# Bidirectional SSD scan on one core: PSUM banks split four and four, state decays given to Pool, row loads, turned-x copies and row scaling moved

## The chip, the cores and the metric

The kernel runs on one core of a Trainium2 chip. The metric is the device time of one execution in microseconds, the median of the runs. PE is TensorE, ACT is ScalarE, DVE is VectorE, Pool is GpSimd, and SP issues the loads of the weights.

## The reference

A first block of a transformer (AdaLN modulation, neighbourhood attention beside a bidirectional state-space scan "SSD", then a mixture of 16 experts), then two plain layers with attention and an MLP. All is fp32, 512 tokens of width 1024, and 256 tokens of context. The change lies in the SSD part, whose core is this:

```python
def _ssd_scan(xs, dt, A, Bm, Cm, h0, return_y):       # 4 groups of 8 heads, head size 64, state 128, chunks of 128
    ...
    states = jnp.einsum('bclgn,bcgrl,bclgrp->bcgrpn', Bc, decay_to_end, x)
    chunk_decay = jnp.exp(a_cs[..., -1]).astype(xs.dtype)
    def step(h, inp):
        dec, st = inp
        return dec[..., None, None] * h + st, h
    ...
    y_diag = jnp.einsum('bcgls,bcgrls,bcsgrp->bclgrp', cb, Lm, x)
    y_off = jnp.einsum('bclgn,bcgrpn,bcgrl->bclgrp', Cc, jnp.moveaxis(h_prev, 0, 1), jnp.exp(a_cs).astype(xs.dtype))
```

Before the scan, the projections of x, B and C pass a convolution over 5 tokens and a SiLU; after it, y is multiplied by SiLU(z) and normalised by root mean square within its group.

## The kernel before

Each engine has a program of its own, and semaphores join them: `up(sem, key)` counts up and names the event, `wait_ge(*at(key))` waits for it. Each engine runs its instructions in the order of its program. The programs are Python generators. `weave(main, filler, per)` mixes two of them at a fixed rate; `pace(main, filler, plan)` mixes them by a list, entry k being how many steps of the filler go ahead of step k of main. All engines use the same mix, so a step of PE has its counterpart on ACT, DVE and Pool.

The 8 banks of PSUM are handed out in turn within a list: `open_bank(pe, key, pool)` takes the bank of that list that was taken longest ago and makes PE wait until its earlier contents are read (the key `free`). Main work takes from `PA = [3, 4, 5, 6, 7]`, filler work from `PG = [0, 1, 2]`.

The SSD runs over groups g = 0 to 3. Main for group g is `*_chunks(g)`, 15 steps:

- Steps 1 to 5 (n = 0 to 4) are the sweep over states. A step has two states, one of each direction; the ten are m = 0 to 9 and are called st0 to st9 here, each one matmul of 128x512 (line 1039). Its right side `xd` is x times a weight (`weigh`, line 1028): even m on DVE, odd m on Pool. DVE then forms the new state as the earlier one times a decay (line 1212) plus the bank (line 1215).
- Steps 6 to 15 (n = 0 to 9) are the output. `act_exponents(n)` makes decay exponents for half a chunk, 8 activations (line 1124) on rows that the ACT queue has loaded from DRAM (`load_rows`, line 1104); `act_decays(n)` takes their exponential (line 1133), after the exponents of n+1; `pool_first` multiplies by C·B (line 1306), which gives M(n); PE's `pe_second(n)` (line 1072) needs M(n). For odd n it also makes the two state terms `yo` (line 1079). `dve_second`, `pool_second` (lines 1316 to 1320) and `dve_join` (line 1277) put y together; the join frees the bank of y.

The filler for group g+1 is `*_proj(g+1)`, 8 steps F1 to F8. F1 to F4 are the convolutions of x, i = 0 to 3. In each, PE projects (line 720, two banks), ACT copies both banks to a padded row (lines 730 and 733), DVE does one product and four multiply-adds (lines 754 and 758), ACT takes SiLU (lines 739 and 742), and PE turns tile i-1 (line 307, two banks), of which DVE copies one part (line 965) and ACT the other (`act_turn_x`, line 935). F5 to F8 make z (line 295, copied with SiLU at line 956). By the rate 0.56 they fall so: steps 1, 2, F1, 3, 4, F2, 5, 6, F3, 7, 8, F4, 9, F5, 10, 11, F6, 12, 13, F7, 14, 15, F8. For group 3 the filler is the q and k projections of two groups of heads (lines 1531 and 1724, copied by ACT at lines 1538 and 1773), and main does its first three steps without filler.

The norm of the group before is finished inside the sweep. `dve_scale_z` and `pool_scale_z` (line 1192) scale its rows by `rstd`, which ACT helps to make (`act_rstd`, lines 327 and 329); PE turns them (`pe_finish`, part 0 and 1), ACT copies the turned tiles (`act_finish`, line 1176) and sends them to DRAM (line 1178, key `yD`). Group 3's own finish comes after its last step and two empty steps. The next stage begins with `PHASE_C`, a wait on all engines but PE for that finish, its last `yD` among the keys; then ACT and DVE copy the tokens into another order (`act_by_blocks`, line 1731, and `dve_by_blocks`, line 1736), on which PE's v projection waits.

Of the kernel before, what the change touches and what calls it, by code (L numbers as in the profile page):

```python
# [178 lines left out]
def build(nc, A, out):  # L179
    ctx = ExitStack()  # L180
    with ctx:
# [66 lines left out]
        PALL, PA, PG = list(range(8)), [3, 4, 5, 6, 7], [0, 1, 2]  # L248
        rings = [PS]
# [476 lines left out]
        def act_conv(act, nm, i, ti, dx, dc, before):  # L726
# [7 lines left out]
                *up(S("act_pad"), ("free", (nm, i, 2)), ("pad", (nm, i))))  # L734
            act.wait_ge(*at("acc", (nm, i)))
# [196 lines left out]
        def act_turn_x(act, g, i):  # L932
            key = ("tx", g, i, 4)
            act.wait_ge(*at("full", key))
            act.activation(xs2[g % 2][:, 4:6, i * 128:(i + 1) * 128], r3(PS.of(key)[:, 0:256], 128), ACT.Copy, bias=0.0, scale=1.0).then_inc(  # L935
                *up(S("act_xs"), ("free", key), ("xs", g, i, 4)))

        def act_proj(act, g):
            for i in range(4):
                prev = ("tx", g, i - 2, 4) if i > 1 else ("tx", g - 1, i + 2, 4)  # L940
                before = [("full", prev)] if g or i > 1 else []
                if g == 0 and i == 1:
                    before = [("full", ("BF", 3, 2))]
                act_conv(act, ("x", g), i, 4 * g + i, xsF[i % 2][:, 0:512], xsF[i % 2][:, 512:768], before)
                if g > 1 and i == 1:
                    act.wait_ge(*at("gone", g - 2, "pool"))
                    act.wait_ge(*at("gone", g - 2, "pe"))
                if i:
                    act_turn_x(act, g, i - 1)
                yield  # L950
# [80 lines left out]
        def pe_chunks(pe, g, pool):  # L1031
            xsT, BT = xs2[g % 2], BT2[g % 2]
            for m, (d, n, c) in enumerate(SWEEP):
# [6 lines left out]
                if d:  # L1040
                    if n in (2, 3) and g:
                        pe_finish(pe, g - 1, n - 2, pool)
                    yield
# [66 lines left out]
        def act_exponents(act, g, n):  # L1110
# [7 lines left out]
            for d in range(2):  # L1118
# [7 lines left out]
                if d == 0:  # L1126
                    for e in range(2):
                        load_rows(act, g, n + 1, e)
# [6 lines left out]
        def act_chunks(act, g):  # L1135
            for d in range(2):
                load_rows(act, g, 0, d)
            for n in range(5):
                if n == 0 and g:
                    act_rstd(act, ("ssd", g - 1), ssy, 4)  # L1140
                if n in (2, 3) and g:
                    act_finish(act, g - 1, n - 2)
                if n == 4:
                    act_exponents(act, g, 0)
                yield
# [48 lines left out]
        def dve_chunks(dve, g):  # L1194
            for m in range(3):
                weigh(dve, 0, g, m)
            for m, (d, n, c) in enumerate(SWEEP):
# [9 lines left out]
                else:  # L1207
                    cd = bc(r3(cdec, 64)[:, c, 32 * d + 8 * g:32 * d + 8 * g + 8], 64)
                    dve.wait_ge(*at("h", g, d, n - 1))
                    if g == 0 and n == 1 and d == 0:  # L1210
                        dve.wait_ge(*at("cd"))
                    dve.tensor_tensor(r3(dst, 64), r3(H_[:, SLOT[d][n - 1], :], 64), cd, ALU.mult).then_inc(*up(S("dve_state")))
                    dve.wait_ge(*at("full", key))
                    dve.wait_ge(*now(S("dve_state")))
                    dve.tensor_tensor(dst, dst, b, ALU.add).then_inc(*up(S("dve_state"), ("free", key), ("h", g, d, n), *keys))
                if d:
                    if n == 0 and g:
# [64 lines left out]
        def pool_chunks(pool, g):  # L1282
            for m in range(3):
                weigh(pool, 1, g, m)
            for m, (d, n, c) in enumerate(SWEEP):
                weigh(pool, 1, g, m + 3)
                if d:
                    if n == 0 and g:
# [1646 lines left out]

        def sp_program(sp):
# [25 lines left out]
        def pe_program(pe):  # L2962
# [31 lines left out]
        def act_program(act):  # L2994
# [9 lines left out]
            weave(main, chain(act_na_qk(act, 0), act_na_qk(act, 1)), 0.57)  # L3004
# [27 lines left out]
        def dve_program(dve):  # L3032
# [10 lines left out]
            weave(main, chain(dve_na_qk(dve, 0), dve_na_qk(dve, 1, 0)), 0.57)  # L3043
# [22 lines left out]
        def pool_program(pool):  # L3066
# [7 lines left out]
            weave(main, chain(pool_na_qk(pool, 0), pool_na_qk(pool, 1)), 0.57)  # L3074
# [58 lines left out]
```

## Time and profile before

| | us |
|---|---|
| median of 3 runs | 4042.74 (4036.76 to 4048.11) |
| the profiled execution | 4034.85 |
| its span, first to last instruction | 4032.9 |
| PE busy | 3663.4 (91%) |
| DVE, ACT, POOL busy | 1137.1, 782.8, 450.8 |
| stretch of the change, first st0 of group 0 to the v projection | 303.9 to 801.2 |

Times in the trace are microseconds from the first instruction. Engine busy times overlap, so they don't add up to the span. The chain that ended last is PE for 53% of the span and DMA for 18%. A row of the timeline gives the start, the length of the run of like instructions, the instruction and its count, and in brackets the idle time ahead of it with what ended it. An fp32 matmul shows as two instructions.

### The profile page before, as it was taken

How to read it: one execution, taken by the hardware profiler on the slowest of the kernel's cores; microseconds unless marked ns; L12 is line 12 of the kernel's file. 1: busy time of each engine (PE TensorE's matmuls, PEld its weight loads, DVE VectorE, ACT ScalarE, POOL GpSimd, SP SyncE). 2: the span in 40 equal slices, each digit the busy share in tenths (PEclk: the TensorE clock that was granted, in tenths of full speed). 3: DMA queues.
4: the chain of work that ended last, by engine and by line, in shares of the span. 5: the costliest groups of instructions: out<-in, count | busy, mean ns of one | idle time of the engine just before them, and what ended most of it. 6: DMA issues, size and time to landing. Idle time of an engine off the chain costs nothing.

```text
span 4032.9 us, 32976 instructions
## 1 busy us (share of the span) xinstructions
PE 3663.4 (91%) x12600; PEld 1762.2 (44%) x12600; DVE 1137.1 (28%) x2594; ACT 782.8 (19%) x1786; POOL 450.8 (11%) x405
## 2 busy tenths in 40 slices
PE   6898888899999888888888888899999999999999
PEld 3354444444444443333233334555444445554444
DVE  2335444434310220311101114443221134432211
ACT  2024344322310210000000003332110123221100
POOL 1001223412100000000000002100221011012210
PEclk8899898999999989999999998999999999999999
DMA  7322223211212569999999992102222120022220
GB/s 253 125 75 75 79 63 94 87 37 50 79 63 88 189 250 409 409 409 409 409 409 409 409 398 73 37 27 84 83 72 80 51 90 32 28 97 69 84 71 34
DMA packets 302153, 634.08 MB, mean 157 GB/s; under 512 B 32499, under 2 KB 145763, under 8 KB 301743
## 3 DMA queue, kind: packets, MB, share of 16 engines
q1 hardware_dynamic: 240480, 591.96, 39.1%
q10 hardware_dynamic: 61519, 40.02, 3.5%
q8 instruction: 102, 1.67, 0.2%
q14 instruction: 52, 0.43, 0.0%
HBM read 625.50 MB, written 10.24 MB: 158 GB/s over the span
## 4 chain that ended last, share of the span: by engine, by line
PE 53%; DMA 18%; DVE 3%; SPq 1%; ACT 1%; issue 1%; POOL 0%; DVEq 0%; ACTq 0%
PE psum L295 26%; DMA arena<-in_w_exp_up_dram 7%; DMA arena<-in_w_exp_gate_dram 7%; PE psum L1531 6%; DMA arena<-in_w_exp_down_dram 4%; PE psum L2799 4%; PE psum L2763 4%; PE psum L2304 4%; PE psum L1359 2%; PE psum L1387 1%; PE psum L2784 1%; PE psum L2253 1%; PE psum L1368 1%; SPq L264 1%; PE psum L2694 1%
## 5 line engine op out<-in xcount | busy, mean ns | idle before, releaser
L295 PE MATMUL psum<-arena 128*128 128x512 f32 (+1 forms) x3200 | 1309.8, 568 | 17.1 <-ACT arena L935 11.9
L295 PEld LDWEIGHTS psum<-arena 128*128 128x128 f32 x3200 | 612.4, 193 | 699.2 <-issue 660.3
L2304 PE MATMUL psum<-arena 128*64 128x512 f32 x3072 | 696.5, 598 | 148.8 <-DMA arena<-in_w_exp_up_dram 76.2
L2304 PEld LDWEIGHTS psum<-arena 128*64 128x64 f32 x3072 | 234.4, 137 | 592.1 <-issue 571.6
L1531 PE MATMUL psum<-arena 128*128 128x512 f32 x768 | 352.8, 614 | 0.0
L720 PE MATMUL psum<-arena 128*128 128x512 f32 (+1 forms) x768 | 274.5, 517 | 1.3 <-ACT arena L538 1.3
L1531 PEld LDWEIGHTS psum<-arena 128*128 128x128 f32 x768 | 147.5, 196 | 193.2 <-issue 192.4
L1465 DVE CUSTOM_DVE_ANT_0 arena<-psum,arena 128x512 f32<-128x512 f32 (+3 forms) x224 | 114.0, 546 | 384.5 <-PE psum L1359 376.3
L2842 POOL TENSOR_SCALAR arena<-arena 128x512 f32<-128x512 f32 x88 | 138.6, 1576 | 696.2 <-ACT arena L2821 696.2
L720 PEld LDWEIGHTS psum<-arena 128*128 128x128 f32 x768 | 152.5, 201 | 125.4 <-issue 114.7
L2848 DVE SCALAR_TENSOR_TENSOR arena<-arena 128x512 f32<-128x512 f32 x88 | 66.2, 752 | 426.6 <-POOL arena L2842 426.6
L1407 ACT ACTIVATE arena<-arena 128x512 f32<-128x512 f32 (+3 forms) x224 | 134.3, 601 | 134.3 <-DVE arena L1465 133.7
L2369 DVE TENSOR_TENSOR arena<-arena,psum 128x512 f32<-128x512 f32 x32 | 22.0, 689 | 462.0 <-PE psum L2304 462.0
L2799 PE MATMUL psum<-arena 128*128 128x512 f32 x352 | 152.0, 592 | 0.0
L2763 PE MATMUL psum<-arena 128*128 128x512 f32 x352 | 151.7, 592 | 0.0
L2821 ACT ACTIVATE arena<-psum 128x512 f32<-128x512 f32 x88 | 52.5, 597 | 509.7 <-PE psum L295 478.2
L1368 PE MATMUL psum<-arena 128*128 128x128 f32 x576 | 85.7, 277 | 55.9 <-DVE arena L1472 30.7
L1542 POOL TENSOR_TENSOR arena<-arena 128x512 f32<-128x512 f32 x48 | 61.3, 1277 | 608.3 <-ACT arena L1538 595.2
L307 PE MATMUL psum<-arena 128*128 128x128 f32 (+3 forms) x442 | 67.6, 300 | 53.4 <-ACT arena L730 18.9
L1368 PEld LDWEIGHTS psum<-arena 128*128 128x128 f32 x576 | 68.4, 142 | 107.6 <-DVE arena L1472 38.1
L2763 PEld LDWEIGHTS psum<-arena 128*128 128x128 f32 x352 | 66.6, 189 | 84.7 <-issue 84.7
L2206 POOL TENSOR_TENSOR arena<-arena 128x128 f32<-128x128 f32 x32 | 12.9, 433 | 809.1 <-PE psum L307 593.2
(276 smaller groups left out, 3022.9 us busy)
## 6 DMA issues: line engine op xcount, KB each, us to landing
arena<-in_w_exp_gate_dram SPq DMA_DIRECT2D x128, 1024.0 KB, 18.6
arena<-in_w_exp_up_dram SPq DMA_DIRECT2D x128, 1024.0 KB, 18.6
arena<-in_w_exp_down_dram SPq DMA_DIRECT2D x128, 1024.0 KB, 18.8
arena<-in_w_in_dram SPq DMA_DIRECT2D x64, 1024.0 KB, 5.3
arena<-in_w_up_dram SPq DMA_DIRECT2D x88, 512.0 KB, 4.8
arena<-in_w_ada_dram SPq DMA_DIRECT2D x24, 1024.0 KB, 7.9
arena<-in_w_down_dram SPq DMA_DIRECT2D x20, 1024.0 KB, 4.9
arena<-acs_scratch ACTq DMA_DIRECT2D x64, 256.0 KB, 4.5
```

The source lines that it names most:

```text
L295: mm = pe.matmul(shaped(b, l, r), l, r, start=kt == 0, stop=kt == nkt - 1)
L307: t = pe.transpose(b[0:m, c * k:(c + 1) * k], x, ident[0:k, 0:k])
L720: mm = pe.matmul(b[:, 0:z - a], wt(nm, kt, 512)[:, i * 128:(i + 1) * 128], HT[:, kt, a:z], start=kt == 0, stop=kt == 7)
L1359: pe.matmul(b[:, 0:u.nk], J.queries(u, a, z), J.keys(u, a, z), start=True, stop=True).then_inc(*up(S("pe_score"), ("full", ("s2", J.id, i, ...
L1368: t = pe.transpose(b[:, 128 * j:128 * j + 128], J.score(i, c)[:, 128 * j:128 * j + 128], ident)
L1407: act.activation(J.score(i, c), J.score(i, c), ACT.Exp, bias=sv2(i, c)[:, 0:1], scale=-1.0, accum_out=sv2(i, c)[:, 1:2]).then_inc(*up(S("a ...
L1465: dve.tensor_tensor_reduce(out=J.score(i, c), in0=PS.of(("s2", J.id, i, c))[:, 0:u.nk], in1=J.table(u, c), scale=-J.scale(u), scalar=3.0e3 ...
L1531: mm = pe.matmul(b, wt(nm, kt, 256)[:, i * 128:(i + 1) * 128], src[:, kt, 0:512], start=kt == 0, stop=kt == 7)
L2304: mm = pe.matmul(banks[n][64 * j:64 * j + 64, :], lhs[:, kt, 64 * j:64 * j + 64], w, start=kt == 0, stop=kt == 2 * nkb - 1)
L2763: mm = pe.matmul(banks[i], actT[:, kt, i * 128:(i + 1) * 128], wt(nm, kt, 512), start=kt == 0, stop=kt == 21)
L2799: mm = pe.matmul(b, actT[:, kt, i * 128:(i + 1) * 128], wt(nm, kt, 512), start=kt == 0, stop=kt == 21)
L2842: pool.tensor_scalar(accs3[n % 4], pads3[n % 4][:, 0:512], w3(L, 0, ti_of(s, i)), None, ALU.mult).then_inc(*up(S("pool_acc"), ("acc3", L, n)))
```

## The change

1. **Banks.** In the four main stretches of the SSD and their fillers the lists are `PA1 = [4, 5, 6, 7]` and `PG1 = [0, 1, 2, 3]`.
2. **State decays.** The product of the earlier state and the decay, 8 per group, is issued by Pool into the new slot, and DVE only adds the bank.
3. **Turned x.** ACT copies its part of turned tile i-1 between the pad copies and the SiLU of convolution i, no longer after the SiLU.
4. **Row scaling and finish.** `act_rstd`, `dve_scale_z` and `pool_scale_z` move from n = 0 to n = 1; `pe_finish` and `act_finish` from n = 2, 3 to n = 3, 4 (on ACT ahead of the exponents of n = 0).
5. **Row loads.** `act_exponents(n)` issues both row loads for n+1 after its 8 activations, no longer after the first 4.
6. **Group 3.** `pace` with `PLAN0` in place of the rate 0.57. F1 to F5 and F7 stay where they were among the steps; F6 goes ahead of step 14, and F8 ahead of the second empty step, so ahead of group 3's finish and no longer behind it.

```diff
+        PA1, PG1 = [4, 5, 6, 7], [0, 1, 2, 3]
...
             act.activation(pad[:, 518:774], PS.of((nm, i, 2))[:, 0:256], ACT.Copy, bias=0.0, scale=1.0).then_inc(
                 *up(S("act_pad"), ("free", (nm, i, 2)), ("pad", (nm, i))))
+            if between:
+                between()
...
-                act_conv(act, ("x", g), i, 4 * g + i, xsF[i % 2][:, 0:512], xsF[i % 2][:, 512:768], before)
...
-                if i:
-                    act_turn_x(act, g, i - 1)
+                act_conv(act, ("x", g), i, 4 * g + i, xsF[i % 2][:, 0:512], xsF[i % 2][:, 512:768], before,
+                         (lambda: act_turn_x(act, g, i - 1)) if i else None)
...
-                    if n in (2, 3) and g:
-                        pe_finish(pe, g - 1, n - 2, pool)
+                    if n in (3, 4) and g:
+                        pe_finish(pe, g - 1, n - 3, pool)
...
-                if d == 0:
-                    for e in range(2):
-                        load_rows(act, g, n + 1, e)
+            for d in range(2):
+                load_rows(act, g, n + 1, d)
...
-                if n == 0 and g:
+                if n == 1 and g:
                     act_rstd(act, ("ssd", g - 1), ssy, 4)
-                if n in (2, 3) and g:
-                    act_finish(act, g - 1, n - 2)
+                if n in (3, 4) and g:
+                    act_finish(act, g - 1, n - 3)
...
-                    dve.tensor_tensor(r3(dst, 64), r3(H_[:, SLOT[d][n - 1], :], 64), cd, ALU.mult).then_inc(*up(S("dve_state")))
                     dve.wait_ge(*at("full", key))
-                    dve.wait_ge(*now(S("dve_state")))
+                    dve.wait_ge(*at("hc", g, d, n))
                     dve.tensor_tensor(dst, dst, b, ALU.add).then_inc(*up(S("dve_state"), ("free", key), ("h", g, d, n), *keys))
...
                 weigh(pool, 1, g, m + 3)
+                if n:
+                    H_ = (hf, hb)[d]
...
+                    pool.wait_ge(*at("h", g, d, n - 1))
...
+                    pool.tensor_tensor(r3(H_[:, SLOT[d][n], :], 64), r3(H_[:, SLOT[d][n - 1], :], 64), cd, ALU.mult).then_inc(
+                        *up(S("pool_hc"), ("hc", g, d, n)))
                 if d:
-                    if n == 0 and g:
+                    if n == 1 and g:
                         pool_scale_z(pool, g - 1)
...
+        PLAN0 = [0, 0] + [1, 0, 1, 0, 1, 0, 1, 1, 1, 0] + [1, 1]
...
-                weave(pe_chunks(pe, g, PA), pe_proj(pe, g + 1, PG), 0.56)
-            main = pe_chunks(pe, 3, PA)
+                weave(pe_chunks(pe, g, PA1), pe_proj(pe, g + 1, PG1), 0.56)
+            main = pe_chunks(pe, 3, PA1)
...
-            weave(main, chain(pe_na_qk(pe, 0, PG), pe_na_qk(pe, 1, PG)), 0.57)
+            pace(main, chain(pe_na_qk(pe, 0, PG1), pe_na_qk(pe, 1, PG1)), PLAN0)
```

## Rows read from the trace of the kernel before

**Rows 1.** Waits of PE, 303 to 801 us: total us, times, longest.

```profile
PE psum L307 <- ACT arena L730: 18.9, 6, 5.7
PE psum L1072 <- POOL arena L1306: 12.1, 8, 2.8
PE psum L295 <- ACT arena L935: 11.9, 3, 4.0
```

**Rows 2.** Timeline of PE, group 1: start, length, instructions, [idle before, releaser].

```profile
444.19 2.08 PE L1039 MATMUL psum<-arena 128*128 128x512 f32 x2 [3.97 <-DVE arena L1215]
...
477.24 0.69 PE L307 MATMUL psum<-arena 128*128 128x128 f32 x2 [5.66 <-ACT arena L730]
478.26 1.94 PE L1072 MATMUL psum<-arena 128*128 128x64 f32 x8 [0.33 <-POOL arena L1306]
...
501.75 8.84 PE L295 MATMUL psum<-arena 128*128 128x512 f32 x16 [3.97 <-ACT arena L935]
...
521.69 1.00 PE L1072 MATMUL psum<-arena 128*128 128x64 f32 x8
...
537.21 1.97 PE L1072 MATMUL psum<-arena 128*128 128x64 f32 x8 [2.76 <-POOL arena L1306]
```

**Rows 3.** Timeline of ACT and its queue in the same stretch.

```profile
448.55 0.69 ACT L1176 ACTIVATE arena<-psum,arena 128x512 f32<-128x512 f32 x1 [0.46 <-ACT arena L1176]
...
466.87 0.94 ACTq L1104 DMA_DIRECT2D arena<-acs_scratch  x2
...
471.20 1.28 ACT L1124 ACTIVATE arena<-arena 128x128 f32<-128x128 f32 x4 [2.07 <-DMA arena<-acs_scratch]
...
476.07 0.63 ACT L1133 ACTIVATE arena<-arena 128x512 f32<-128x512 f32 x1
```

**Rows 4.** Timeline of DVE in the same stretch.

```profile
437.88 4.86 DVE L758 SCALAR_TENSOR_TENSOR arena<-arena 128x772 f32<-128x772 f32 x4
...
460.05 4.20 DVE L758 SCALAR_TENSOR_TENSOR arena<-arena 128x772 f32<-128x772 f32 x4
...
504.59 0.69 DVE L1277 TENSOR_TENSOR arena<-psum,arena 128x512 f32<-128x512 f32 x1 [2.47 <-POOL arena L1320]
...
522.00 0.69 DVE L1277 TENSOR_TENSOR arena<-psum,arena 128x512 f32<-128x512 f32 x1 [6.20 <-POOL arena L1320]
```

**Rows 5.** Groups of instructions, 303 to 801 us: busy us, mean ns | idle.

```profile
L1028 POOL TENSOR_TENSOR arena<-arena 128x512 f32<-128x512 f32 x18 | 22.3, 1254 | 33.7 <-PE psum L1039 33.7
L1212 DVE TENSOR_TENSOR arena<-arena 128x512 f32<-128x512 f32 x32 | 22.2, 695 | 0.0
...
L1192 POOL TENSOR_SCALAR arena<-arena 128x512 f32<-128x512 f32 x8 | 13.6, 1708 | 27.2 <-DVE arena L322 27.2
```

**Rows 6.** Timeline of PE at the start of group 3.

```profile
689.54 2.05 PE L1039 MATMUL psum<-arena 128*128 128x512 f32 x2 [6.18 <-POOL arena L1028]
...
697.46 7.03 PE L1531 MATMUL psum<-arena 128*128 128x512 f32 x16
...
715.77 1.10 PE L1072 MATMUL psum<-arena 128*128 128x64 f32 x8 [2.59 <-POOL arena L1306]
```

**Rows 7.** Timeline of POOL at the start of group 3.

```profile
684.65 3.39 POOL L1192 TENSOR_SCALAR arena<-arena 128x512 f32<-128x512 f32 x2 [7.25 <-DVE arena L322]
```

**Rows 8.** Timeline of PE at the end of group 3.

```profile
784.00 3.65 PE L307 MATMUL psum<-arena 128*128 128x128 f32 x16 [8.00 <-POOL arena L1192]
...
801.23 14.00 PE L295 MATMUL psum<-arena 128*128 128x512 f32 x32 [1.58 <-issue]
```

**Rows 9.** Timeline of ACT and its queue at the end of group 3.

```profile
776.03 0.39 ACT L1773 ACTIVATE arena<-psum 128x256 f32<-128x256 f32 x1 [2.85 <-PE psum L1724]
...
789.82 0.33 ACTq L1178 DMA_DIRECT2D yT_scratch<-arena  x1
...
798.91 0.64 ACT L1731 ACTIVATE arena<-arena 128x512 f32<-128x512 f32 x1
```

**Rows 10.** DMA issues of the whole run: count, KB each, median us to landing.

```profile
yT_scratch<-arena ACTq DMA_DIRECT2D x16, 256.0 KB, 2.0
```

More of the change, by code:

```diff
@@ L724, in pe_conv, with act_conv @@
                 mm.then_inc(*up(S("pe_conv"), *keys))
-        def act_conv(act, nm, i, ti, dx, dc, before):
+        def act_conv(act, nm, i, ti, dx, dc, before, between=None):
             pad, prev = pads1.take((nm, i))
@@ L933, in act_turn_x @@
             key = ("tx", g, i, 4)
+            if g > 1 and i == 0:
+                act.wait_ge(*at("gone", g - 2, "pool"))
+                act.wait_ge(*at("gone", g - 2, "pe"))
             act.wait_ge(*at("full", key))
@@ L943, in act_proj @@
                     before = [("full", ("BF", 3, 2))]
-                act_conv(act, ("x", g), i, 4 * g + i, xsF[i % 2][:, 0:512], xsF[i % 2][:, 512:768], before)
-                if g > 1 and i == 1:
-                    act.wait_ge(*at("gone", g - 2, "pool"))
-                    act.wait_ge(*at("gone", g - 2, "pe"))
-                if i:
-                    act_turn_x(act, g, i - 1)
+                act_conv(act, ("x", g), i, 4 * g + i, xsF[i % 2][:, 0:512], xsF[i % 2][:, 512:768], before,
+                         (lambda: act_turn_x(act, g, i - 1)) if i else None)
                 yield
@@ L1207, in dve_chunks @@
                 else:
[L1208 to L1211, printed above, removed]
-                    dve.tensor_tensor(r3(dst, 64), r3(H_[:, SLOT[d][n - 1], :], 64), cd, ALU.mult).then_inc(*up(S("dve_state")))
                     dve.wait_ge(*at("full", key))
-                    dve.wait_ge(*now(S("dve_state")))
+                    dve.wait_ge(*at("hc", g, d, n))
                     dve.tensor_tensor(dst, dst, b, ALU.add).then_inc(*up(S("dve_state"), ("free", key), ("h", g, d, n), *keys))
                 if d:
-                    if n == 0 and g:
+                    if n == 1 and g:
                         dve_scale_z(dve, g - 1)
@@ L1286, in pool_chunks @@
                 weigh(pool, 1, g, m + 3)
+                if n:
+                    H_ = (hf, hb)[d]
+                    cd = bc(r3(cdec, 64)[:, c, 32 * d + 8 * g:32 * d + 8 * g + 8], 64)
+                    pool.wait_ge(*at("h", g, d, n - 1))
+                    if g == 0 and n == 1 and d == 0:
+                        pool.wait_ge(*at("cd"))
+                    elif n == 1 and d == 0:
+                        pool.wait_ge(*at("gone", g - 1, "pe"))
+                    pool.tensor_tensor(r3(H_[:, SLOT[d][n], :], 64), r3(H_[:, SLOT[d][n - 1], :], 64), cd, ALU.mult).then_inc(
+                        *up(S("pool_hc"), ("hc", g, d, n)))
                 if d:
-                    if n == 0 and g:
+                    if n == 1 and g:
                         pool_scale_z(pool, g - 1)
@@ L3003, in act_program @@
                 next(main)
-            weave(main, chain(act_na_qk(act, 0), act_na_qk(act, 1)), 0.57)
+            pace(main, chain(act_na_qk(act, 0), act_na_qk(act, 1)), PLAN0)
             wait_all(act, PHASE_C)
@@ L3042, in dve_program @@
                 next(main)
-            weave(main, chain(dve_na_qk(dve, 0), dve_na_qk(dve, 1, 0)), 0.57)
+            pace(main, chain(dve_na_qk(dve, 0), dve_na_qk(dve, 1, 0)), PLAN0)
             dve_na_rope(dve, 1, 3)
@@ L3073, in pool_program @@
                 next(main)
-            weave(main, chain(pool_na_qk(pool, 0), pool_na_qk(pool, 1)), 0.57)
+            pace(main, chain(pool_na_qk(pool, 0), pool_na_qk(pool, 1)), PLAN0)
             pool_near_zero(pool)
```

## The prediction

> **What bounds the kernel now.** I read first who made PE wait in the stretch of the change. Most of it falls on the second turn after a convolution (18.9 us), on the products with M (12.1 us), and on the first z projection (11.9 us) [rows 1]; 8.0 us more fall once on the row scaling of group 3 [rows 8]. That is 50.9 us, and the smaller entries of that view bring it to some 67, all that a better order could give. The question is whether these waits are causes or only the places where PE meets a later one.
>
> The timeline of PE in group 1 answers that. The turn waits 5.66 us for a bank until 477.24, and the next instruction, the first product with M, waits again, until 478.26 [rows 2]. M(0) comes from Pool, which follows the exponential that ACT ended at 476.70 [rows 3]. So a free bank would let PE turn 5.66 us earlier and then stand before the same M(0) until 478.26. The z projection waits 3.97 us until 501.75; that wait is ended by an ACT copy that comes late only because it stands behind a SiLU. The last product with M in the group waits for Pool until 537.21 [rows 2]. What sets the group's length is therefore ACT: exponents, row load, exponents, exponential, pad copies, DVE's convolution, SiLU, and again. The reader is to see that PE's bank waits lie inside that chain's shadow, and that ACT itself waits 2.07 us for a row load in it [rows 3].
>
> **The change, part by part.** I cost a group of the middle (1 or 2) by its effect on that chain.
>
> *Banks four and four.* The turn's wait goes, and M(0) takes its place: nothing. The z projection no longer waits for ACT; it may start near 498 and end near 505 to 507. What is late next is the join: with four main banks, y of chunk c+1 takes the bank of y of chunk c, which the join frees. Joins start at 504.59 and 522.00 [rows 4] and take 0.69. The second one ends at 522.7, after PE's use at 521.69 [rows 2]: a new wait of 1.0 us there. Alone, this part is worth 0 to -2 us a group, since the last M at 537.2 still ends it; bounds -4 (all of the z wait) and +1.
>
> *Turned x earlier.* Each of three copies (128x256) leaves the way from SiLU to the next exponents. The like copy of 128x256 at 776.03 took 0.39 us [rows 9], so I take -1 us on the chain; bounds 0 and -1.2.
>
> *Decays by Pool.* DVE sheds 8 products of 0.695 us, Pool gains 8 of about 1.25 us (the weighing product has the same operands) [rows 5]. Pool idles before M in the middle groups, so its time is covered by convolution 0. On DVE the last earlier product before the state add that PE waits for at 444.19 [rows 2] goes: -0.8 us. Against it stands the meeting of both engines. The four multiply-adds took 4.86 us with one Pool product beside them and 4.20 us without [rows 4], 0.66 us for each Pool instruction, and now about three lie there instead of one: +1.3 us. Finish part 1 leaves this place on PE (-0.9 us). Convolution 1 starts 0.5 to 1 us earlier; bounds -2 and +1.
>
> The page "SBUF — State Buffer" of the Trainium skill, section "SBUF: two separate sides", says that Pool and a DVE instruction with two SBUF inputs hold the shared ports by an exclusive lock for a whole instruction. By that rule each Pool product could cost DVE its full length, about 1.25 us in place of 0.66, and both middle groups together would be some 2.5 us slower than my sum; rows 4 show about half of it.
>
> *Finish a step later.* ACT now copies and sends tiles 2 and 3 after the SiLU of convolution 1 and directly ahead of the exponents of n = 0. A copy takes 0.69 us and 0.46 us of issue go ahead of it, 1.15 together [rows 3]: +2.3 us on the chain, where before they lay in ACT's wait for PE. Bounds 0 and +2.5.
>
> *Row loads after eight activations.* The load for the next exponents was issued at 466.87 after four activations, and the next exponents began at 471.20 when it had landed, 4.33 us later [rows 3]. Now it is issued four activations later, 1.28 us [rows 3], and lands that much later. Where two calls of exponents follow each other (n = 0 and 1, 2 and 3, 5 and 6) the second waits. +1.3 us for the first pair; the others had little or no wait before and about as much reserve as they need, so +1 each. Bounds 0 (if rows land in under 3 us) and +4 for the three.
>
> Sum on ACT at M(0): -0.8 - 0.4 + 2.3 + 1.3 = +2.4 us. At M(3) and at the join of chunk 1 it is +2 to +3; the z projection's earlier start is used up there. At the group's end I take +2 us for groups 1 and 2 each. Group 0 has no finish: +0.5 us. New also: the C·B product of n = 0 takes st8's bank in groups 1 and 2, which DVE frees only after convolution 1, so PE waits near 4 us before convolution 2. That is covered, since PE had over 5 us of wait behind it.
>
> *Group 3, start.* Here nothing covers Pool, for the sweep runs three steps without filler. Before, Pool started the row scaling at 684.65 [rows 7], and st5 waited 6.18 us for Pool's weighing behind it [rows 6]. That wait goes. But rstd now follows the adds of step 2, and these wait for Pool's two products after one weighing: 3.5 us later, so Pool scales from 688.1 to 691.5 (two of 1.708 us [rows 5]) and weighs st7 until 692.8. Behind it stand in Pool's order two decays, a weighing and two decays: 5 x 1.25 = 6.3 us, 699.0. DVE adds 0.7, which frees the bank of st9; with st9 and finish part 1, 2 us, the filler starts at 701.7 and not at 697.46 [rows 6]: +4.2 us. ACT's exponents then have finish part 1 before them and a chain of row loads with no convolution between, +1.3 us a link, so M(1), for which PE waits until 715.77 [rows 6], comes at about 723. I take +7 us at F3, from where PE was full until the end of F7; bounds +3 and +12 (M(3) or M(5) late too, when a load is slow).
>
> *Group 3, end.* PE's idle 8.0 us before the finish [rows 8] looks as if F8 now filled it. It does not: ACT makes rstd in order after its copy of F7's last bank at 776.03 [rows 9], and 8 us later PE starts. With F8 ahead, ACT's copy of F8 is ahead of rstd, so the 8 us come again after F8. F7, F8, 8 us and 3.65 us of turns end where F7, 8 us, turns and F8 ended. But now nothing lies between the turns and the v projection. The last yD was issued 5.8 us after the turns began at 784.00 [rows 8, 9] and needs 2.0 us to land [rows 10]; the v projection started 2.3 us after the first of ACT's copies for the new token order at 798.91 [rows 8, 9]. So v starts about 10.2 us after the turns start, or 29.3 us after F7 ended at 776.0, where it was 25.2 us (801.23) [rows 8]. +4 us; bounds -8 (if the 8 us are filled) and +6.
>
> **Sum.** 0.5 + 2 + 2 + 7 + 4 = +15.5 us. Against the profiled execution, 4034.85 us with 4032.9 in its span and 2 around it, that gives 4050.4. The median of the runs shown is 7.9 us above the profiled execution, so I put the same sum on the median: 4042.7 + 15.5 = 4058.2. Past 801 us PE is busy nearly without a break, so I let nothing be given back later. A change of 0.3% is 12 us, and less than that can't be told from no change.
>
> **Rivals.**
> *A, the loads are hidden and group 3 recovers.* If rows land fast enough, the links' +1.3 us vanish: about -1 in group 0, -2 in groups 1 and 2, -4 in group 3. +15.5 - 9 = +6.5, 4049 us. For it: the second pair of a middle group showed no wait. Against: the 2.07 us wait of [rows 3]. Chance 0.2.
> *B, banks are the bound, faster.* If PE's z wait is real and ACT keeps up, the 11.9 us [rows 1] go, and z, which took 8.84 us after its wait [rows 2] where a like run of 16 took 7.03 [rows 6], gives 1.8 us in each of three groups: -17 us, 4026. It decides from the point where M(3) is ready when PE has done z, that is 2 us earlier than now. Against it stand the added ACT work and the later loads. Chance 0.14.
> *C, slow loads everywhere in group 3.* With the chain of loads bare, PE waits at M(3), M(5) and M(7) too, 4 us each, and cold restarts come on top: +15.5 + 15 = +30, 4073. Chance 0.1.
> *The change doesn't do what it says:* the bank waits move to M and to the joins. That is part of the forecast.
> The forecast itself, +8 to +24 us, has 0.56. Of it about a tenth part lies under +12.
>
> Faster by over 0.3%: 0.14, from B. Slower: 0.60, from the forecast's larger part and C. Within: 0.26, from A and edges. The range reaches from 4036 to 4074 us; the forecast's own is 4051 to 4067.
>
> **What the profile after would show.** PE's wait for a pad copy at the turn and for the turned-x copy at z are gone; waits for M grow, and new ones appear for the join before y and for a state add before C·B. ACT's waits for row loads grow from one in group 1 to two or three. Pool's scaling in group 3 starts near 688, the filler near 702, the v projection near 816. Wrong would I be if M(0) of group 1 came no later than now, or if F8 were followed by less than 8 us of idle.

## The result, and the profile after

The changed kernel took 4059.18 us (median of 6 runs, 4054.51 to 4061.2), the kernel before in runs beside it 4041.98 us. The ratio is 1.0042, 95% interval 1.0029 to 1.0055: slower, by more than 0.3% in the ratio itself, with the interval's lower end just under that. The forecast was 4058.2 us. The profiled execution has a span of 4055.0 us, 22.1 us more than before.

I cut the stretch of the change at events that every kernel has: the first state product of each group, the first and third runs of the filler in group 3 (F1, F3), the end of F7, and the start of the v projection. Lengths in us, each from one profiled execution. The last two columns are the timed median and the estimated ratio to the kernel before, which ran beside each set: its medians were 4037.61 us beside e1 to e4, 4035.95 beside e5 to e8 and 4036.68 beside e9 to e12. The ratio is an estimate from all runs and not the quotient of the two medians; the two differ by up to 0.0008.

| kernel | group 0 | group 1 | group 2 | to F1 | F1 to F3 | F3 to F7's end | F7 to v | sum | median | ratio |
|---|---|---|---|---|---|---|---|---|---|---|
| before | 118.9 | 126.8 | 129.3 | 18.6 | 22.4 | 56.2 | 25.2 | 497.3 | 4041.98 | |
| after | 119.2 | 127.2 | 129.9 | 21.7 | 29.0 | 55.9 | 28.6 | 511.5 | 4059.18 | 1.0042 |
| e1_banks | 113.9 | 125.7 | 125.4 | 18.5 | 23.5 | 62.3 | 24.9 | 494.2 | 4034.01 | 0.9998 |
| e2_rows_mid | 116.6 | 125.9 | 127.0 | 21.7 | 25.0 | 56.1 | 28.6 | 501.0 | 4046.74 | 1.0028 |
| e3_scale_early | 116.9 | 128.6 | 127.0 | 20.9 | 23.7 | 55.8 | 28.6 | 501.3 | 4050.89 | 1.0041 |
| e4_rate | 117.0 | 129.4 | 129.0 | 21.7 | 26.7 | 62.9 | 24.9 | 511.6 | 4057.63 | 1.0056 |
| e5_decays | 119.0 | 126.8 | 126.0 | 19.9 | 22.3 | 55.8 | 24.7 | 494.4 | 4035.57 | 1.0000 |
| e6_turn | 116.0 | 122.8 | 123.3 | 18.4 | 25.6 | 56.2 | 25.2 | 487.4 | 4028.37 | 0.9980 |
| e7_cover | 119.0 | 126.7 | 129.2 | 18.6 | 25.2 | 56.5 | 23.3 | 498.4 | 4041.94 | 1.0013 |
| e8_cover_banks_turn | 116.5 | 126.1 | 126.6 | 18.2 | 23.2 | 55.8 | 23.3 | 489.6 | 4033.91 | 0.9993 |
| e9_no_rows_no_scale | 116.5 | 126.8 | 126.0 | 20.9 | 20.6 | 55.8 | 28.6 | 495.1 | 4044.82 | 1.0019 |
| e10_turn_decays | 115.9 | 122.6 | 123.4 | 19.9 | 23.2 | 56.6 | 25.5 | 487.1 | 4026.43 | 0.9977 |
| e11_rows_late | 122.5 | 129.7 | 129.7 | 18.5 | 27.0 | 55.8 | 24.8 | 508.0 | 4047.03 | 1.0024 |
| e12_scale_late | 119.2 | 129.4 | 126.9 | 20.1 | 25.0 | 55.8 | 24.8 | 501.2 | 4041.38 | 1.0011 |

Two warnings for this table. From group 0 to F3 of group 3, after and e4_rate are the same program, yet the groups of e4_rate differ by -2.1, +2.2 and -0.9 us and its part from F1 to F3 by -2.3; over all of it e4_rate is 3.2 us shorter. Before and e7_cover are the same program there too: their groups agree to 0.1 us, but e7_cover is 2.8 us longer from F1 to F3. So a single part means little under some 2.8 us and the sum little under some 3. And the stretch of after grew by 14.1 us, its span by 22.1.

What PE waited for, 303 to 816 us (total us, times, longest), against [rows 1]:

```profile
PE psum L1074 <- POOL arena L1312: 24.6, 8, 6.5
PE psum L1074 <- DVE arena L1273: 18.0, 6, 3.4
PE psum L308 <- DVE arena L1211: 8.1, 3, 4.0
PE psum L308 <- POOL arena L1193: 8.0, 1, 8.0
PE psum L1055 <- DVE arena L1211: 6.9, 2, 3.4
PE psum L1041 <- POOL arena L1030: 6.6, 1, 6.6
...
PE psum L308 <- ACT arena L731: 0.8, 2, 0.5
```

The wait for a pad copy at the turn fell from 18.9 us to 0.8, and the z projection's 11.9 us are gone from the list. In their place stand the products with M behind Pool (24.6 us where it was 12.1), the new wait for the join before y (18.0 us in six waits, L1074 behind the join of L1273), and a new one for the state add before C·B (6.9 us). The wait for a state add at the turn (8.1 us) is the one that stood at 444.19 in [rows 2], one instruction later. This is the picture of a wait that is renamed: the banks are free, and PE stands before what comes next on the chain.

PE in group 1, against [rows 2]:

```profile
445.68 2.23 PE L308 MATMUL psum<-arena 128*128 128x128 f32 x8 [3.95 <-DVE arena L1211]
...
465.53 0.49 PE L1055 MATMUL psum<-arena 128*128 128x128 f32 x2 [3.43 <-DVE arena L1211]
465.85 12.18 PE L721 MATMUL psum<-arena 128*128 128x512 f32 x32
...
481.97 1.08 PE L1074 MATMUL psum<-arena 128*128 128x64 f32 x8 [3.29 <-POOL arena L1312]
...
499.77 7.04 PE L296 MATMUL psum<-arena 128*128 128x512 f32 x16
510.24 1.80 PE L1074 MATMUL psum<-arena 128*128 128x64 f32 x8 [3.43 <-DVE arena L1273]
...
539.40 2.08 PE L1074 MATMUL psum<-arena 128*128 128x64 f32 x16 [3.28 <-DVE arena L1273]
```

M(0) at 481.97 is 57.6 us after the group's first state product (424.37); before it was 478.26 after 422.84, 55.4 us. The z projection now starts with no wait and takes 7.04 us instead of 8.84, as rival B had it; then PE idles 3.43 us before the join lets y go on (510.24, the first join of the group). C·B at 465.53 waits for a state add, 3.43 us, in both middle groups.

ACT in the same place, against [rows 3]:

```profile
468.20 2.45 ACT L1126 ACTIVATE arena<-arena 128x128 f32<-128x128 f32 x8 [0.46 <-ACT arena L1177]
470.68 0.94 ACTq L1106 DMA_DIRECT2D arena<-acs_scratch  x2
475.07 2.44 ACT L1126 ACTIVATE arena<-arena 128x128 f32<-128x128 f32 x8 [4.42 <-DMA arena<-acs_scratch]
...
479.79 0.63 ACT L1134 ACTIVATE arena<-arena 128x512 f32<-128x512 f32 x1
```

Read it from the top: eight exponents without a break, directly behind the last finish copy, then both loads issued together at 470.68, and the next exponents 4.42 us of idle later. Before, the load went out after four exponents and the idle time was 2.07 us.

DVE and Pool at the first convolution of group 1, against [rows 4, 5]:

```profile
439.42 5.52 DVE L761 SCALAR_TENSOR_TENSOR arena<-arena 128x772 f32<-128x772 f32 x4
...
460.67 4.20 DVE L761 SCALAR_TENSOR_TENSOR arena<-arena 128x772 f32<-128x772 f32 x4
```

```profile
436.93 1.04 POOL L1030 TENSOR_TENSOR arena<-arena 128x512 f32<-128x512 f32 x1
437.93 2.35 POOL L1291 TENSOR_TENSOR arena<-arena 128x512 f32<-128x512 f32 x2
440.24 1.76 POOL L1030 TENSOR_TENSOR arena<-arena 128x512 f32<-128x512 f32 x1
```

Group 3 on PE, with Pool at its start and ACT at its end, against [rows 6 to 9]:

```profile
681.49 5.32 PE L1041 MATMUL psum<-arena 128*128 128x512 f32 x12
...
695.22 2.04 PE L1041 MATMUL psum<-arena 128*128 128x512 f32 x2 [6.63 <-POOL arena L1030]
...
703.21 7.03 PE L1537 MATMUL psum<-arena 128*128 128x512 f32 x16
...
719.58 1.08 PE L1074 MATMUL psum<-arena 128*128 128x64 f32 x8 [2.25 <-POOL arena L1312]
...
726.92 1.97 PE L1074 MATMUL psum<-arena 128*128 128x64 f32 x8 [5.99 <-POOL arena L1312]
...
732.20 7.09 PE L1537 MATMUL psum<-arena 128*128 128x512 f32 x16
...
794.79 3.61 PE L1730 MATMUL psum<-arena 128*128 128x256 f32 x16
806.40 3.65 PE L308 MATMUL psum<-arena 128*128 128x128 f32 x16 [8.00 <-POOL arena L1193]
...
816.67 16.18 PE L296 MATMUL psum<-arena 128*128 128x512 f32 x32 [5.16 <-DVE arena L1742]
```

```profile
690.68 3.39 POOL L1193 TENSOR_SCALAR arena<-arena 128x512 f32<-128x512 f32 x2 [3.88 <-DVE arena L323]
...
695.04 2.04 POOL L1291 TENSOR_TENSOR arena<-arena 128x512 f32<-128x512 f32 x2
...
698.49 4.04 POOL L1291 TENSOR_TENSOR arena<-arena 128x512 f32<-128x512 f32 x4
```

```profile
812.22 0.33 ACTq L1179 DMA_DIRECT2D yT_scratch<-arena  x1
814.34 0.65 ACT L1737 ACTIVATE arena<-arena 128x512 f32<-128x512 f32 x1 [2.15 <-DMA yT_scratch<-arena]
```

Pool scales 9.2 us after the first state product of the group (690.68 - 681.49), where it was 5.8 before, and the filler starts 21.7 us after it instead of 18.6. PE's wait for a weighing by Pool is still there (6.63 us, 6.18 before), but two state products later, before st7 and not st5. PE waits 2.25 us for M(0) at 719.58 and 5.99 us for M(1) at 726.92, so F3 comes at 732.20. At the end F8 stands ahead of the idle 8.00 us, which are as long as they were, and the v projection starts at 816.67, 4.4 us after the last yD was issued. Its first 32 matmuls take 16.18 us, where they took 14.00 before [rows 8]: the 5.16 us of idle ahead of them came with a clock that was lower at their start, as the last section shows.

### The profile page after: what moved, and what is told of

It is laid out like the page before. It is cut to its first block, busy times and chain, and to the rows that moved or that the text cites. A ratio compares the mean times of both kernels' runs of the same rounds, so it can differ in the third digit from the quotient of the medians.

```text
span 4055.0 us, 32979 instructions
## 1 busy us (share of the span) xinstructions
PE 3668.7 (90%) x12600; PEld 1765.1 (44%) x12600; DVE 1122.5 (28%) x2562; ACT 783.0 (19%) x1786; POOL 487.3 (12%) x437
## 4 chain that ended last, share of the span: by engine, by line
PE 52%; DMA 18%; DVE 3%; ACT 1%; issue 1%; POOL 0%; SPq 0%; DVEq 0%; ACTq 0%
PE psum L296 26%; DMA arena<-in_w_exp_up_dram 7%; DMA arena<-in_w_exp_gate_dram 7%; PE psum L1537 6%; DMA arena<-in_w_exp_down_dram 4%; PE psum L2805 4%; PE psum L2769 4%; PE psum L2310 4%; PE psum L1365 2%; PE psum L2790 1%; PE psum L1393 1%; PE psum L2259 1%; PE psum L1374 1%; PE psum L2228 1%; PE psum L2700 1%
## 5 line engine op out<-in xcount | busy, mean ns | idle before, releaser
L296 PEld LDWEIGHTS psum<-arena 128*128 128x128 f32 x3200 | 612.4, 193 | 687.5 <-issue 658.6
L1537 PEld LDWEIGHTS psum<-arena 128*128 128x128 f32 x768 | 147.4, 196 | 193.4 <-issue 192.5
L1471 DVE CUSTOM_DVE_ANT_0 arena<-psum,arena 128x512 f32<-128x512 f32 (+3 forms) x224 | 113.9, 546 | 385.3 <-PE psum L1365 381.4
L721 PEld LDWEIGHTS psum<-arena 128*128 128x128 f32 x768 | 153.5, 203 | 127.3 <-issue 116.6
L1374 PEld LDWEIGHTS psum<-arena 128*128 128x128 f32 x576 | 69.4, 143 | 107.9 <-DVE arena L1478 38.1
L308 PE MATMUL psum<-arena 128*128 128x128 f32 (+3 forms) x442 | 65.8, 296 | 44.0 <-DMA arena<-in_conv_w_dram 15.5
L1365 PE MATMUL psum<-arena 64*128 64x512 f32 (+6 forms) x448 | 105.1, 551 | 0.0
## 6 DMA issues: line engine op xcount, KB each, us to landing
arena<-in_w_exp_up_dram SPq DMA_DIRECT2D x128, 1024.0 KB, 18.6
arena<-in_w_exp_down_dram SPq DMA_DIRECT2D x128, 1024.0 KB, 18.6
```

The costliest lines, as they stand in the source:

```text
L296: mm = pe.matmul(shaped(b, l, r), l, r, start=kt == 0, stop=kt == nkt - 1)
L721: mm = pe.matmul(b[:, 0:z - a], wt(nm, kt, 512)[:, i * 128:(i + 1) * 128], HT[:, kt, a:z], start=kt == 0, stop=kt == 7)
L1365: pe.matmul(b[:, 0:u.nk], J.queries(u, a, z), J.keys(u, a, z), start=True, stop=True).then_inc(*up(S("pe_score"), ("full", ("s2", J.id, i, ...
L1374: t = pe.transpose(b[:, 128 * j:128 * j + 128], J.score(i, c)[:, 128 * j:128 * j + 128], ident)
L1471: dve.tensor_tensor_reduce(out=J.score(i, c), in0=PS.of(("s2", J.id, i, c))[:, 0:u.nk], in1=J.table(u, c), scale=-J.scale(u), scalar=3.0e3 ...
L1537: mm = pe.matmul(b, wt(nm, kt, 256)[:, i * 128:(i + 1) * 128], src[:, kt, 0:512], start=kt == 0, stop=kt == 7)
```

## The experiments

**Banks four and four alone.**

```
-weave(pe_chunks(pe, g, PA), pe_proj(pe, g + 1, PG), 0.56)
+weave(pe_chunks(pe, g, PA1), pe_proj(pe, g + 1, PG1), 0.56)
-main = pe_chunks(pe, 3, PA)
+main = pe_chunks(pe, 3, PA1)      # and PG1 for the q and k filler
```

> The kernel before, with the banks four and four alone. My theory: ACT's chain sets a group's length, so the turn's wait for a pad copy (18.9 us in all) moves to M(0) and the z wait (11.9 us) to M(3) and the joins; each group 0 to 2 us shorter, total 0 to -6 us, not told from no change. Rival (banks are the bound): -17 us or more, and the waits of PE in the stretch fall from 67 us to under 50.

The ratio is 0.9998 (0.9989 to 1.0007): no change. The three groups are 5.1, 1.1 and 3.9 us shorter, 10.0 together and more than expected, but group 3 gives 6.2 back between F3 and the end of F7:

```profile
751.90 1.41 PE L1073 MATMUL psum<-arena 128*128 128x64 f32 x8 [4.58 <-DVE arena L1278]
753.10 8.51 PE L1532 MATMUL psum<-arena 128*128 128x512 f32 x16
...
764.06 7.03 PE L1532 MATMUL psum<-arena 128*128 128x512 f32 x16
```

The join before y costs 4.58 us there, and the filler run behind it takes 8.51 us, where the next one takes 7.03. Rival B, banks as the bound, falls: they give a little and bring this wait, and PE's waits in the stretch don't fall but grow from 67.8 us to 72.1. The banks also have a price that I had put at nothing. With four main banks st6 needs one that DVE frees only behind convolution 0, so PE runs st6 and st7 together where st6 ran ahead before [rows 2]:

```profile
440.44 4.07 PE L1040 MATMUL psum<-arena 128*128 128x512 f32 x4 [4.83 <-DVE arena L1216]
```

M(0) of group 1 comes 57.1 us after the group's first state product in this kernel, 1.7 us later than before, with nothing changed but the banks.

**Row loads back in the middle of the exponents** (the change without that part).

```
-            for d in range(2):
-                load_rows(act, g, n + 1, d)
+                if d == 0:
+                    for e in range(2):
+                        load_rows(act, g, n + 1, e)
```

> The changed kernel with the row loads of n+1 issued again after the first four activations. From the first st0 of group 3 to F3 the changed kernel took 50.7 us (before 40.9). My theory: three links of row loads are bare there, each 1.3 us shorter again, so 46 to 47 us; groups 0 to 2 each 1 to 2 us shorter; total -6 to -10 us against the changed kernel. Rival (only the later row scaling costs): 50 us in that stretch and under 2 us in all.

The stretch is 10.5 us shorter, with 46.8 us from st0 to F3 as the theory had it, and the ratio is 1.0028 (1.0015 to 1.0041) in place of 1.0042 (1.0029 to 1.0055). ACT's waits for row loads, of after and of this kernel (total us, times, longest):

```profile
ACT arena L1126 <- DMA arena<-acs_scratch: 30.4, 22, 4.4
```

```profile
ACT arena L1126 <- DMA arena<-acs_scratch: 12.5, 9, 2.3
```

**Scaling and finish a step earlier** (the change without that part).

```
-    if n in (3, 4) and g:  act_finish(act, g - 1, n - 3)
+    if n in (2, 3) and g:  act_finish(act, g - 1, n - 2)
-    if n == 1 and g:       act_rstd(...)       # dve_scale_z, pool_scale_z too
+    if n == 0 and g:       act_rstd(...)
```

> The changed kernel with row scaling, turns and copies of the finish back at their earlier steps. My theory: in group 3 the filler starts about 4 us after where it does now less, so st0 to F3 takes 45 to 47 us instead of 50.7, since st5 waits for Pool again by 6 us but the tail of decays is shorter; groups 1 and 2 get 2 us shorter each; total -7 to -9 us. Rival (the row loads cost all of it): under 2 us in all.

10.1 us shorter in the stretch, with F1 to F3 5.3 us shorter; the time stays at 1.0041 (1.0026 to 1.0057). By medians it is 13.3 us above its kernel before, where the changed kernel is 17.2 above. So the trace has a gain that the timed runs bear out in small part at most. Some of it can't come from the edit: group 0 has no finish, yet it is 2.3 us shorter, and group 1, where 2 us less were expected, is 1.4 us longer.

**Group 3's filler by rate, not by the list** (the change without that part).

```
-pace(main, chain(...), PLAN0)
+weave(main, chain(...), 0.57)      # on all four engines
```

> The changed kernel with the rate 0.57 in group 3 in place of the list. My theory: F8 lies between the turns and the v projection again; from the end of F7 to the v projection 25 us instead of 28.6, the 8.0 us idle before the turns stay; total -3.4 us. Rival (the list fills the 8 us and its cost is elsewhere): the stretch grows to 33 us or more.

The tail is as expected, 24.9 us, but the total is not: the sum is the change's, 511.6 against 511.5, and the ratio 1.0056 (1.0040 to 1.0071). The terms cancel: F3 to F7's end +7.0, F7 to v -3.7, and -3.2 up to F3, where the program is the same and the difference is scatter. The join's wait of e1_banks is back, 4.58 us before a filler run of 8.48. In the changed kernel F6 stands ahead of that wait and hides it. I had costed this move at nothing.

**State decays by Pool alone.**

```
-dve.tensor_tensor(r3(dst, 64), r3(H_[:, SLOT[d][n - 1], :], 64), cd, ALU.mult)
+pool.tensor_tensor(r3(H_[:, SLOT[d][n], :], 64), r3(H_[:, SLOT[d][n - 1], :], 64), cd, ALU.mult)
```

> The kernel before, with the state decays by Pool alone. My theory: in groups 0 to 2 nothing sets the end but ACT's chain, so each group changes by less than 1 us; in group 3 the filler starts 1 to 3 us later (18.6 us from st0 before), since Pool's decays stand behind its row scaling. Total 0 to +4 us. Rival (DVE's sweep is the bound there): groups 0 to 2 each 1 us or more shorter, total -3 us.

Ratio 1.0000 (0.9989 to 1.0011), -2.9 us in the stretch, which is within the scatter; group 3's filler starts 1.3 us later, as the theory had it, and group 2 is 3.3 us shorter, which it had not. The four multiply-adds take 5.52 us here too, so that loss belongs to this part; the time shows nothing of it.

**Turned x earlier alone.**

```
+            if between:
+                between()          # act_turn_x of the convolution before
             act.wait_ge(*at("acc", (nm, i)))
```

> The kernel before, with the copies of turned x between the pad copies and the SiLU alone. With three filler banks the z wait on PE was ended by the copy behind the SiLU. Theory: the copy comes about 6 us earlier, so the z waits (11.9 us in three groups) go, but the group's end is set by M(7), so each group is 0.5 to 2 us shorter, total -2 to -6 us. Rival: the z wait was a true bound, -12 us and more. Second rival: no change, less than 1 us.

0.9980 (0.9971 to 0.9989): faster than before, and by more than the theory's 2 to 6 us: 10.0 in the stretch, 7.6 in the medians. PE's waits, to be read beside [rows 1]:

```profile
PE psum L1073 <- POOL arena L1307: 20.7, 11, 2.8
PE psum L307 <- ACT arena L730: 16.9, 5, 5.4
PE psum L307 <- POOL arena L1193: 8.0, 1, 8.0
```

No wait for z is left in that view and none for the join has come, while the wait at the turn is nearly as large as before (18.9 us). The groups are 3.0, 4.0 and 6.0 us shorter.

**The 8 us at group 3's end covered.** Before, with F8 ahead of the turns on PE and with rstd and the scaling ahead of F8 on the other engines.

```
-    yield from idle(2)
     act_rstd(act, ("ssd", g), ssy, 4)     # dve_scale_z, pool_scale_z too
+    yield from idle(2)
```

> The kernel before, with the list of the change in group 3, and rstd and row scaling of group 3 issued ahead of F8 on ACT, DVE and Pool. Theory: F8 on PE now covers the 8.0 us of idle before the turns; from the end of F7 to the v projection 21 to 22 us where it was 25.2 before and 28.6 in the change. Total -3 to -4 us, which the timing alone can't tell from no change but the stretch can. Rival (the tail is set by something else than rstd): the idle before the turns stays at 4 us or more.

The 8 us are gone and 10.13 us stand in their place, one instruction later:

```profile
790.21 1.91 PE L307 MATMUL psum<-arena 128*128 128x128 f32 x16
...
803.30 15.74 PE L295 MATMUL psum<-arena 128*128 128x512 f32 x32 [10.13 <-DVE arena L1736]
```

```profile
796.97 0.69 ACT L1176 ACTIVATE arena<-psum,arena 128x512 f32<-128x512 f32 x1 [4.29 <-DMA yT_scratch<-arena]
...
798.84 0.33 ACTq L1178 DMA_DIRECT2D yT_scratch<-arena  x1
```

The turns follow F8 without a break, but ACT's last yD is issued at 798.84, and the copies for the new token order need it. From F7 to v it is 23.3 us, 2.0 less than before, where 3 to 4 less were expected. The time did not follow: 1.0013 (1.0004 to 1.0022), slower than before. The first run of v takes 15.74 us behind that idle time, 14.00 before, which takes back 1.7 of the 2.0; the rest of the loss stays open.

**Cover, banks and turned x together.** The three edits above in one kernel.

> Run 7's kernel with the banks four and four and the copies of turned x earlier, and so none of the decays by Pool, later row loads and later finish. With banks alone the three mixed groups were 9.8 us shorter together, and group 3 lost 6.2 us to the join in its rate; the list puts F6 ahead of that use. Theory: groups -10 to -12 us, no join wait at step 14 of group 3, tail -3.8 us: -12 to -16 us against the kernel before. Rival (the list does not hide the join wait): -6 us.

0.9993 (0.9983 to 1.0003). The groups sum to 369.2 us, where banks alone gave 365.0 and turned x alone 362.0: both take away the same wait at z, so they don't add, and the banks' wait for the join stays (14.6 us, all in groups 0 to 2). That is argued from the waits. The theory's 12 to 16 us are missed: the stretch is 7.7 us shorter. The rival's reason is not it, for the list does hide the join's wait in group 3 (55.8 us from F3 to F7's end, 62.3 with banks alone).

**The change with row loads and scaling as before** (the edits of e2_rows_mid and e3_scale_early together).

> The changed kernel without its later row loads and without its later scaling and finish; banks, decays, turned x and the list stay. Singly, taking back the loads shortened the stretch by 10.5 us and taking back the scaling by 10.1. Theory: the two costs lie one behind the other on ACT and Pool, so they add: stretch 491 to 496 us (change 511.5, before 497.3), kernel at or under the time before. Rival (each hides the other's wait): stretch over 500 us.

The stretch is 495.1 us, 16.3 less than the change and 2.2 less than before, as expected. The time is 1.0019 (1.0009 to 1.0028), still slower, where the kernel was to be at or under the time before. So the two parts explain about half of the 0.42%, and the stretch doesn't explain the rest.

**Turned x and decays.** e6_turn and e5_decays in one kernel.

> The kernel before with turned x earlier and the state decays by Pool, nothing else. Alone turned x shortened the stretch by 10.0 us and the decays by 2.9. Theory: they touch different waits and add, stretch 483 to 486 us, about -10 to -13 us against before and the fastest so far. Rival: the decays' gain was scatter of the clock, stretch 487 to 489 us, the time that of turned x alone.

0.9977 (0.9968 to 0.9985), 4026.43 us against 4036.68. This is the fastest version run. The stretch is 487.1 us, which is the rival's figure and not the theory's: the decays add nothing to turned x, and by the intervals the two kernels can't be told apart.

**Late row loads alone.** The edit of e2_rows_mid the other way, on the kernel before.

> The kernel before with the row loads after eight activations, nothing else. Theory: every pair of exponents without a convolution between waits 1.3 us longer, so groups 0 to 2 gain 1 to 3 us each in length, and group 3 from F1 to F3 gains 4 us or more; stretch +7 to +12 us. Rival (loads only cost beside the later finish): under +3 us.

1.0024 (1.0014 to 1.0034), +10.7 us in the stretch, as expected. ACT waits for loads nearly as long as in the changed kernel, where before it was 12.3 us in 7 waits:

```profile
ACT arena L1124 <- DMA arena<-acs_scratch: 27.9, 21, 4.3
```

**Late scaling and finish alone.** The edit of e3_scale_early the other way, on the kernel before.

> The kernel before with row scaling, turns and copies of the finish one step later, nothing else. Theory: groups 1 and 2 +2 us each by ACT's two copies before the exponents; group 3 from st0 to F1 +1 to +3 us and F1 to F3 +3; stretch +7 to +11 us; group 0 unchanged. Rival (it costs only beside the decays by Pool and the late loads): under +4 us.

1.0011 (1.0002 to 1.0020), +3.9 us in the stretch, little more than the scatter. The theory's 7 to 11 us are missed, and the rival's figure, under 4 us alone, is met.

## Why the prediction was right

*The chain and not the banks.* Right as to the waits and the time: pad and z waits left, waits for M and for the join came, and e1_banks gives no change. M(0) of group 1 moved by +2.2 us where the sum on ACT said +2.4, but that agreement is partly luck. Singly, at that M(0): banks +1.7 us (forecast 0), row loads +0.9 (+1.3), finish +0.6 (+2.3), decays -0.3 (-0.8), turned x -0.4 (-0.4). These come from single executions; the same program differed there by 0.1 us (before, e7_cover) and by 1.0 (after, e4_rate).

*Row loads.* Right in mechanism and in place: 22 waits for a load where there were 7, 30.4 us instead of 12.3, and five in group 1 where I said two or three. The price was low. I took 1.3 + 1 + 1 us a group and a link of 1.3 us in group 3; alone it costs 10.7 us (e11_rows_late) and taken back it gives 10.5 (e2_rows_mid). It is the largest single cost of the change, and the one whose price alone the timed runs show most clearly (1.0024).

*Finish a step later.* I said +2.3 us a middle group, and the share in group 3's start. Alone +3.9, taken back -10.1, both with some 3 us of scatter and the second with 2.3 us in group 0 that aren't its own. So it seems to cost more when the loads are late too; the timed runs, +0.11% alone and no change when taken back, don't show that. Both taken back give 16.3 in the stretch.

*Decays by Pool.* The meeting was costed at +1.3 us on the multiply-adds, with three Pool products beside them in place of one; they took 5.52 us, +0.66 against [rows 4]. Two lie there and not three: from 439.42 to 442.0 Pool ran a decay's end and a weighing, 2.6 us, and DVE lost 1.32 us against its unburdened 4.20. Pool's part of the meeting I had left out: its product at 440.24 took 1.76 us beside them and 1.04 at 436.93. With DVE idle a decay takes 1.02 us (2.04 for two) and a weighing 1.04; the 1.25 that I took for both was a mean with DVE's work beside it. The whole part is worth nothing that can be measured (1.0000). The rule of the Trainium skill's page "SBUF — State Buffer", section "SBUF: two separate sides", that the loser is blocked for a whole instruction, would by my estimate have the two engines lose together what they overlap, here 2.6 us. The trace has 1.32 us on DVE, 0.72 on the weighing and 0.31 on the pair of decays (2.35 us where two took 2.04), 2.35 in all, which is near that. With the single weighing of before (1.24 us at 438.56) it was 0.66 and 0.20, less than the overlap, so the trace doesn't settle the rule. It does show that both engines lose, where I had put the whole loss on DVE.

*Turned x earlier.* Mis-sized. I took -1 us a group, bounds 0 to -1.2, as three short copies on ACT; alone it gives 3.0 to 6.0. I had read the 11.9 us before z as lying in the shadow of ACT's chain. e6_turn shows otherwise: z's 11.9 us go, the waits for M grow from 12.1 us to 20.7 only, and the group ends sooner. So one half of rival B was true, that z's wait is real; moving the copy removes it without a new wait, while more banks remove it and bring the join's.

*Banks.* The groups gave 5.1, 1.1 and 3.9 us, where my bounds were -4 and +1. The join's new wait was forecast once a group at 1.0 us, behind the second join; in the changed kernel it is six waits of 2.0 to 3.4 us, 18.0 in all, behind the first and the third join of each group. The y behind the second one starts without a wait (525.35). I had taken the join's end from the times of before. But the join stands behind convolution 3 on DVE, and in group 1, counted from the first state product, it ends at 82.4 us before, 84.1 with banks alone and 85.8 in the changed kernel, while PE now gets through z sooner. With banks alone the same six waits are 15.1 us.

*The groups' sum.* Forecast +0.5, +2, +2; measured +0.2, +0.4, +0.6, all within the scatter of a group. The gains were larger and the costs too.

*Group 3.* F1 3.2 us later (forecast 4.2), M(1) 8.6 later (forecast 7.2), F3 9.8 later (forecast 7, bounds 3 to 12). The same program in e4_rate has M(1) 6.4 and F3 7.5 later, so the overrun isn't clear of scatter. Rival C's waits at M(3), M(5) and M(7) didn't come: after M(1) PE waits for no M in this group. F7 to v +3.4 (forecast +4), with the 8.00 us after F8 and the v projection at 816.67, both as said. From the turns' start to v it was 10.3 us (816.67 - 806.40), forecast 10.2. F6's move, which I had left out of the sum, is worth 7.0 us, for without it the join costs that much there (e4_rate). And past the start of v I let nothing change: its first run is 2.2 us longer.

*The sum.* +15.5 us forecast, +14.1 in the stretch, +17.2 in the medians. The direction and the main cost were right. That the total came out so near, 4058.2 against 4059.18 us, is partly luck: several terms were wrong in opposite directions (turned x and banks gave more, loads and join cost more), and a single stretch scatters by 3 us.

*What stays open.* The parts run singly (banks -3.1, decays -2.9, turned x -10.0, scaling +3.9, row loads +10.7) sum to -1.4 us, the list gives -0.1 (after against e4_rate), and the whole is +14.1. The row loads and scaling account for 16.3 us of stretch when taken back together; why the gains of banks and turned x, which overlap, are so nearly gone in the rest is argued here from the waits and not shown.

Also open in part is the time behind the start of v, where the instructions are the same. The span less the start of v is 3231.7 us before (4032.9 - 801.23), 3238.3 after (4055.0 - 816.67) and 3243.5 in e9_no_rows_no_scale (4044.4 - 800.90); over all fourteen profiles it lies between these ends, and e5_decays, whose time is that of the kernel before, has 3240.1. So much of it looks like scatter of single executions. One piece is not: all six kernels with the list (after, e2, e3, e7, e8, e9) come to v with 5.0 to 10.1 us of idle and take 15.7 to 16.9 us for its first 32 matmuls, and all eight without it come with 1.6 us of idle and take 14.00. The list thus costs 1.7 to 2.9 us that the stretch doesn't show. Still more seems to be handed on: the timed median, less 1.9 us around the span and less the profile's start of v, is 3240.6 to 3242.1 us in after, e2, e3 and e9, and 3232.2 to 3238.8 in the others. What in the common parts of those four does that was not separated. It may be why the times of e3_scale_early and e9_no_rows_no_scale are worse than their stretches.

## What to carry to other kernels

Before you cost a wait at nothing because it lies in a longer chain's shadow, follow what its removal lets start earlier: here an ACT copy moved ahead of an independent wait gave 0.2% for a few lines of code. Issue a load at the first moment when its buffer allows, for a load held back by four activations came back as 22 waits where there were 7. When banks are shared out anew, look for the slowest reader of the ring that shrinks (here DVE's join behind Pool), and check in the last stage, where no other work hides it. And before you read a difference of 2 or 3 us from two profiles, compare a part of them that has the same program.

## What the runs showed of the hardware

The run of 32 matmuls behind C·B has the same idle time of 3.43 us ahead of it in groups 1 and 2, and takes 12.18 us in one and 10.49 in the other. The windows of PE over both (busy us, granted clock, DMA share, GB/s):

```profile
465.85:477.87 12.02, 12.02 (x34) 0.86 0.27 87
594.29:604.62 10.33, 10.33 (x35) 1.00 0.31 103
```

These are means of a level that changes: in group 1 the clock fell from 2.4 to 1.2 GHz (1.00 to 0.50 of full speed) at the start of the run and was back at 2.4 GHz some 3 us later, in group 2 it stayed at 2.4.

```profile
462.10:465.50 3.40, 0.00 (x0) 1.00 0.00 0
467.00:468.00 1.00, 1.00 (x2) 0.50 0.54 207
471.00:472.00 1.00, 1.00 (x4) 1.00 0.12 35
```

So a group's length moves by 1.7 us with no difference in the program, which is the size of several terms that I argued about. The first run of v shows the same: behind 5.16 us of idle the clock stood at 0.50 from 816.7 to 821 us and at 1.00 from 823, and the run took 16.18 us; before, behind 1.58 us of idle, it stood at 1.00 and the run took 14.00.

Pool's product of 128x512 takes the same time as a decay and as a weighing when DVE is idle, 1.02 and 1.04 us. Beside DVE's work the weighing took up to 1.76 us, its mean was 1.32 in the changed kernel, and the mean of the decays was 1.09. Each engine lost time to the other where they met.
